# Routing's long VectorE operations as four operations of 512 columns each

## What is computed

```python
def peer_ffn(x, w_q, subkeys, u_tab, v_tab):
    ...
        q = jnp.einsum('td,de->te', xb, w_q).reshape(PEER_BLOCK, PEER_HEADS, 2, PEER_DQ // 2)
        s = jnp.einsum('thpc,hpkc->thpk', q, subkeys).astype(F32)
        v1, i1 = lax.top_k(s[:, :, 0], PEER_TOPK)
        v2, i2 = lax.top_k(s[:, :, 1], PEER_TOPK)
        cand = (v1[..., :, None] + v2[..., None, :]).reshape(PEER_BLOCK, PEER_HEADS, PEER_TOPK * PEER_TOPK)
        cidx = (i1[..., :, None] * N_KEYS + i2[..., None, :]).reshape(PEER_BLOCK, PEER_HEADS, PEER_TOPK * PEER_TOPK)
        top_s, sel = lax.top_k(cand, PEER_TOPK)
        eidx = jnp.take_along_axis(cidx, sel, axis=-1).reshape(PEER_BLOCK, PEER_HEADS * PEER_TOPK)
        gates = jax.nn.softmax(top_s, axis=-1).reshape(PEER_BLOCK, PEER_HEADS * PEER_TOPK)
        h = jax.nn.gelu(jnp.einsum('td,ted->te', xb, u_tab[eidx]).astype(F32))
        w = (gates * h).astype(xb.dtype)
        return jnp.einsum('te,ted->td', w, v_tab[eidx])
```

## Time and profile before

| | |
|---|---|
| median of three runs | 2377.19 us |
| profiled execution | 2383.61 us, of which the traced span is 2381.8 us |
| TensorE, VectorE, ScalarE, GpSimd busy | 95%, 70%, 55%, 42% of the span |
| mean granted clock of TensorE | 0.98 |
| routing of layer 0 | about 382 to 521 us of the span |
| routing of layer 1 | about 1540 to 1678 us of the span |

### The profile page before, as it was taken

One profiled execution on the slowest core, in us unless ns is written; L12 is line 12 of the kernel. 1 busy time (PEld: TensorE's weight loads), 2 busy tenths in 40 slices (PEclk: granted clock), 3 DMA queues, 4 the chain that ended last, 5 costly groups with the idle time before them and its releaser, 6 DMA issues. The chain is left out here.

```text
span 2381.8 us, 45623 instructions
## 1 busy us (share of the span) xinstructions
PE 2252.8 (95%) x15467; PEld 2037.0 (86%) x15467; DVE 1657.9 (70%) x3385; ACT 1305.5 (55%) x2954; POOL 1010.3 (42%) x777
## 2 busy tenths in 40 slices
PE   7788899999999999999989898999999998999998
PEld 7678699999999977888878787999999997778886
DVE  4756478979888555666646555899698884566666
ACT  4314365447776555555546544644677764555554
POOL 4603346997777620000033253499877774000000
PEclk9899999999999999999989899999999999999999
DMA  6339544444444475555545493444544446555553
GB/s 225 133 114 262 226 168 147 163 159 151 142 142 139 153 241 168 188 188 186 185 136 160 142 358 130 158 152 159 168 142 139 144 138 205 191 186 188 188 185 124
DMA packets 115506, 409.28 MB, mean 172 GB/s; under 512 B 20025, under 2 KB 22241, under 8 KB 110049
## 3 DMA queue, kind: packets, MB, share of 16 engines
q1 hardware_dynamic: 111328, 391.45, 49.7%
q0 software_dynamic: 4032, 15.86, 2.0%
HBM read 397.11 MB, written 10.14 MB: 171 GB/s over the span
## 5 line engine op out<-in xcount | busy, mean ns | idle before, releaser
L1988 POOL TENSOR_TENSOR slab_ring_lo<-slab_ring,u_hi 128x512 fp32r<-128x512 f32 x512 | 714.1, 1414 | 200.6 <-ACT u_hi L2082 199.9
L2030 PE MATMUL banks<-operand_hi,u_hi 128*128 128x264 f32 x2048 | 594.6, 290 | 18.6 <-POOL slab_ring_lo L1988 18.4
L2032 PE MATMUL banks<-operand_hi,slab_ring_lo 128*128 128x264 f32 x2048 | 583.1, 285 | 0.0
L2031 PE MATMUL banks<-operand_lo,u_hi 128*128 128x264 f32 x2048 | 581.9, 284 | 0.0
L308 POOL TENSOR_TENSOR slab_ring_lo<-slab_ring,slab_hi 128x512 fp32r<-128x512 f32 x130 | 175.3, 1350 | 701.2 <-ACT slab_hi L298 701.1
L2432 DVE TENSOR_TENSOR operand_lo<-slab_ring,operand_hi 128x512 fp32r<-128x512 f32 x512 | 352.9, 692 | 132.9 <-ACT operand_hi L2397 123.4
L2480 PE MATMUL banks<-operand_hi,w_hi 128*128 128x512 f32 x1024 | 409.9, 400 | 12.9 <-DVE w_lo L2428 12.6
L2082 ACT ACTIVATE u_hi<-slab_ring 128x512 fp32r<-128x512 f32 x512 | 322.6, 632 | 162.1 <-PE banks L2032 162.0
L2481 PE MATMUL banks<-operand_hi,w_lo 128*128 128x512 f32 x1024 | 407.3, 398 | 0.0
L2482 PE MATMUL banks<-operand_lo,w_hi 128*128 128x512 f32 x1024 | 407.2, 398 | 0.0
L2030 PEld LDWEIGHTS banks<-operand_hi,u_hi 128*128 128x128 f32 x2048 | 386.6, 189 | 23.3 <-POOL slab_ring_lo L1988 19.2
(11 more groups left out here) (396 smaller groups left out, 3927.8 us busy)
## 6 DMA issues: line engine op xcount, KB each, us to landing
slab_ring<-in_u SPq DMA_DIRECT2D x256, 512.0 KB
slab_ring<-in_v SPq DMA_DIRECT2D x256, 512.0 KB
slab_ring<-in_proj SPq DMA_DIRECT2D x144, 512.0 KB
cache_k_T<-in_cache_k SPq DMA_DIRECT2D x16, 1024.0 KB, 7.9
cache_v<-in_cache_v SPq DMA_DIRECT2D x16, 1024.0 KB, 13.2
memory_T<-in_mem POOLq DMA_DIRECT2D x2, 1024.0 KB, 5.0
sample_state<-in_state POOLq DMA_DIRECT2D x1, 2048.0 KB, 8.2
out_mem_k_out<-mem_k_T SPq DMA_DIRECT2D x16, 128.0 KB, 2.9
```

Source lines behind the costliest of these rows:

```text
L1988: nc.gpsimd.tensor_tensor(step.ring_lo[:, s, g * HC:(g + 1) * HC, :], step.slab(s)[:, g * HC:(g + 1) * HC, :], hi[:, buf].bitcast(F32), AL ...
L2030: nc.tensor.matmul(bank, hi[:, buf, k, :], xh[:, c, :], start=(c == 0), stop=False)
L2031: nc.tensor.matmul(bank, hi[:, buf, k, :], xl[:, c, :], start=False, stop=False)
L2032: last = nc.tensor.matmul(bank, step.ring_lo[:, s, c, :], xh[:, c, :], start=False, stop=(c == DC - 1))
```

## The change

The operations L2184, L2213 and L2216 of `route`, each over all heads of a tile, are written as operations over two heads each: four of 512 columns in place of one of 2048. The sums, comparisons and products are the same. Within a four no instruction waits for the one before it, and only the last counts up the semaphore that `link` waits for. With one head (decoded tokens) there is one part of 256 columns as before.

```diff
                 v4 = val[:, 0:NQ].rearrange("p (h q) n -> p h q n", q=2)
-                shape = [P, heads, TOPK, TOPK]
-                link(nc.vector.tensor_tensor(cand[:, H].rearrange("p h (a b) -> p h a b", a=TOPK),
-                                             v4[:, :, 0, :].unsqueeze(3).to_broadcast(shape),
-                                             v4[:, :, 1, :].unsqueeze(2).to_broadcast(shape), ALU.add))
+                PART = min(heads, 2)
+                parts = [slice(h, h + PART) for h in range(0, heads, PART)]
+                shape = [P, PART, TOPK, TOPK]
+                for some in parts:
+                    last = nc.vector.tensor_tensor(cand[:, some].rearrange("p h (a b) -> p h a b", a=TOPK),
+                                                   v4[:, some, 0, :].unsqueeze(3).to_broadcast(shape),
+                                                   v4[:, some, 1, :].unsqueeze(2).to_broadcast(shape), ALU.add)
+                link(last)
...
-                    wide = [P, heads * TOPK, TOPK]
-                    link(nc.vector.tensor_tensor(eq, partf[:, H].rearrange("p h n -> p (h n)").unsqueeze(2).to_broadcast(wide),
-                                                 step.iota[:, 0:TOPK].unsqueeze(1).to_broadcast(wide), ALU.is_equal))
-                    e4 = cand[:, H].rearrange("p h (k a) -> p h k a", k=TOPK)
-                    link(nc.vector.tensor_tensor(e4, e4, idxf[:, H, half, :].unsqueeze(2).to_broadcast(shape), ALU.mult))
+                    wide = [P, PART * TOPK, TOPK]
+                    for some in parts:
+                        last = nc.vector.tensor_tensor(
+                            cand[:, some].rearrange("p h (k a) -> p (h k) a", k=TOPK),
+                            partf[:, some].rearrange("p h n -> p (h n)").unsqueeze(2).to_broadcast(wide),
+                            step.iota[:, 0:TOPK].unsqueeze(1).to_broadcast(wide), ALU.is_equal)
+                    link(last)
+                    for some in parts:
+                        e4 = cand[:, some].rearrange("p h (k a) -> p h k a", k=TOPK)
+                        last = nc.vector.tensor_tensor(e4, e4, idxf[:, some, half, :].unsqueeze(2).to_broadcast(shape), ALU.mult)
+                    link(last)
                     link(nc.vector.reduce_sum(chosen(half), eq, axis=AX))
```

## The result

| | before | after |
|---|---|---|
| median (six runs each) | 2378.49 us | 2390.34 us |
| lowest and highest | 2376.36, 2382.19 | 2387.06, 2391.59 |
| profiled execution, its span | 2383.61, 2381.8 | 2391.13, 2389.4 |

The ratio is 1.0047, 95% interval 1.0037 to 1.0057: the changed kernel is slower by 11.2 us (8.8 to 13.6), or by 11.9 between the medians. The forecast was 2395, +18.1.

A forecast was written before the change was run, and what follows sets the result against it. TensorE was taken to bound the kernel. Routing ending 7.15 and 6.95 us late in the two layers gave +14.1 us, TensorE's clock +4.0: +18.1 on 2377.2, so 2395 us, range 2374 to 2404 (8 in 10).

The forecast's parts named there:

- What bounds the kernel: TensorE sets the `u` loop's pace; smaller pieces can win at most 8 to 9 us a layer of GpSimd's lateness.
- Strict turns: In routing, each 512-column piece alternates with one GpSimd subtraction, 1.72 us a piece; chance 0.64.
- rival (A): Routing still ends in time, at under 1.12 us a piece; TensorE keeps 6 to 7 us a layer: 2364, chance 0.12.
- VectorE, +34 us a layer: 40 pieces in routing take 68.8 us in place of 32, less 2.8 for pieces that find GpSimd idle.
- rival (C): VectorE keeps its turn through all four pieces, 2.52 us a group; slack hides most: 2380, chance 0.14.
- The decoded tile, -7.6: At routing's end GpSimd is idle, so eight operations no longer wait: 2.1 us in place of 9.7.
- The deadline: ScalarE's first exponential at 540.05 leaves routing 19.25 us of slack; routing ends 7.15 us past it, delaying TensorE whole.
- The swallowed gain: TensorE reaches slab 48's end 4 to 6 us earlier, then only waits longer before slab 50.
- The gap of 1.3 us per tile: TensorE gap behind GpSimd expected to remain at each tile's second pair of operations, about 1.3 us.
- The clock, +2.0 a layer: After some 10 us idle before slab 50, TensorE restarts at half rate and loses 2.0 us a layer.
- (B): VectorE wins some turns, pieces going in twos, L1988 near 2.4 us; lengthening 14 us stays in the slack: 2373, chance 0.10.

The follow-up runs named there:

- late deadline: Exponentials moved from behind slab 47 to behind slab 55: pieces of 512 took 2375.42 us, whole operations 2387.15; ratios to the kernel before 0.9978 and 1.0021.

## Why the prediction was right

**What bounds the kernel.** Right. GpSimd's lateness was what smaller pieces could win, and the runs with the late deadline and with PSUM show it as TensorE's time. The pieces won some 6 us in layer 0 before slab 48 where the deadline was late, as many as I had; the 8 to 9 us that I put at the most were not reached by pieces, and PSUM, which removes the turns themselves, won 10.1.

**Strict turns.** Right in the sign and nearly in the price: 1.70 us a piece where the sum took 1.72. The two L1137 of the earlier trace rows, at 1.13 and 1.21, were the misleading neighbours of rival (A): the GpSimd operation between them was a shorter one.

**VectorE, +34 us a layer.** A term that was mis-sized: 30.9. From start to the start of what follows, the ten groups took 63.3 us (eight of L2218 and L2225 in 54.6, two of L2187 in 6.2 and 2.5) in place of 32.4. Strict turns throughout would be 68.2, so 4.9 were saved where I took off 2.8 for pieces that find GpSimd idle. 4.3 of them are tile 1's pair sums, where VectorE kept its turn through all four as in rival (C). GpSimd came from idleness there: behind TensorE's wait at slab 28 it had stood for 6.2 us until 476.45, and then for 0.54. I had read its idle time only between 399 and 449 us, which does not cover tile 1. That one group fell out so was luck, since what decides it is open.

**The decoded tile, -7.6.** It gave 6.8 (17.1 to 10.3 us). Of the eight waits that I took off, L2187's 1.23 us was still there: GpSimd worked until 537.6 and not until 536.

**The deadline.** The mechanism and its place were right. From slab 0 on, the lengthening is 31.0 - 6.8 = 24.2 us, the slack was 19.25, and the exponential is 5.0 us late where I had 7.15. ScalarE stood for 7.5 us at it and TensorE for 5.3 and 1.15, where I had 11 and 10, since routing ended 3.0 us sooner than in my sum and ScalarE was there at 536.7 and not at 535.

**The swallowed gain.** Right in its effect, wrong in its size: TensorE reached slab 48 only 2.6 us earlier, not 4 to 6. The step that failed is the list of who waits for routing. I followed the path to the exponentials and overlooked that L2017 waits for tile 1's first pass. The wait and the half rate behind it cost 2.7 + 1.6 us a layer. The deadline at the exponential swallowed them, so the sum did not feel it, and that was luck: with pieces in the first tile alone they took all that the pieces had won. The gap of 1.3 us per tile that I had left to the pieces did not come at all.

**The clock, +2.0 a layer.** Mis-sized: 0.6. The gross cost was as I had it, 2.3 us between slabs 50 and 52. But 1.7 of it came back by slab 56. Before, VectorE's one-hots delayed GpSimd there and TensorE had its gap of 1.46 us at 558.43; after, the gap does not arise. That TensorE's own lateness prevents it is not shown: with PSUM the gap is missing in layer 0 too, where TensorE was not late. I had cost this neighbourhood at nothing, and it held a gain.

Together: 5.0 + 0.6 in place of 7.15 + 2.0 a layer, so 11 us in place of 18. The signs of all terms held; the lengthening and the clock were sized too large.

**The rivals.** (A) is excluded by the turns, (B) by L1988, which is nowhere near 2.4 us. (C) is what happened in one group of ten, and did not in the other nine.

## What to carry to other kernels

Splitting a long operation does not give the neighbour its turn earlier for nothing: where the other engine always has work waiting, every piece buys one more turn of it, here 1.17 us each. So count pieces times turns, and compare with the slack at every place that waits for any part of the split work, not only for its end; a size in between (here 1024 columns) may take most of the gain and stay within it. Better still, remove the contention: one input of each long operation in PSUM (and with it the output of the casts) was worth 23 us, twice as much as the split cost, whatever the size of the pieces.

## What the runs showed of the hardware

- The price of a turn is very regular: beside GpSimd's 128x512 subtraction, 1.17 us and 1.04 ns a column from 256 to 2048 columns. Comparison, product and subtraction, plain and fp32r output lie on the same line.
- Turns are not given by one rule. GpSimd nearly always got the next one, but in 35 of 49 cases in which it was idle when VectorE's series of four began and came into its first or second piece, and in one in which it came straight behind its own operation, it was passed over to the end of the series: 2.07 to 2.10 us in place of 1.28 beside L477, 3.29 to 3.59 beside fours of 512 columns.
- TensorE's granted clock fell to 0.51 for 3.4 us behind a wait of only 2.67 us (L2017 at 470.54), and to 0.50 for 10.2 us behind one of 5.29 and one of 1.15. The short wait cost 1.6 us more than its length. It does not do so each time: in layer 1 of the pieces with the later deadline L2017 waited 2.67 us as well (1624.91), and the clock stayed at 1.00.
- With one input in PSUM two engines that took 3.26 and 3.31 us beside each other take 2.29 and 1.27. A short operation that was left as it was still waited there: the split of the positions (L2212 in that kernel), with its one input and its output in SBUF, took 1.32 us, and 0.21 where it found no neighbour (the same operation is L2213 of after, at 423.47). No TensorE gap came of it.
